# Moving the second half's norm, a spill of the residual and three weight tiles in a two-layer trunk on one Trainium2 core

## The reference

```python
x = x + g2[:, None, :] * y                      # end of layer 0
hk = _modulate(_rmsnorm(x, kv_norm_g), kv_shift, kv_scale)
k_all, v_all = jnp.split(hk @ kv_w, 2, axis=-1)
...
q = (h @ b_w_q[j]).reshape(B, S, N_HEADS, HEAD_DIM)
o = _stick_breaking(q, k_shared, v_shared)      # 16 heads of 64
y = o.transpose(0, 2, 1, 3).reshape(B, S, D) @ b_w_out[j]
x = x + g1[:, None, :] * y
```

## Time and profile before

| | |
|---|---|
| Time, median of 3 runs | 2663.4 us (2663.28 to 2665.89) |
| Profiled execution, its own time | 2662.75 us |
| Its span, first to last instruction | 2661.0 us |
| PE busy | 2573.8 us (97%) |
| DVE busy | 1438.4 us (54%) |
| ACT busy | 956.9 us (36%) |
| POOL busy | 149.4 us (6%) |
| Mean granted TensorE clock | 0.987 |

### The profile page before, as it was taken

How to read it: one execution, slowest core, us unless ns; L and a number is a source line. 1 busy time by engine, 2 the same in 40 slices (tenths; PEclk the granted TensorE clock), 3 DMA queues, 4 the chain that set the end, 5 groups by cost and what they waited for, 6 DMA issues and landing times.

```text
span 2661.0 us, 36194 instructions
## 1 busy us (share of the span) xinstructions
PE 2573.8 (97%) x13680; PEld 2159.2 (81%) x13680; DVE 1438.4 (54%) x1742; ACT 956.9 (36%) x1513; POOL 149.4 (6%) x152
## 2 busy tenths in 40 slices
PE   6999999999999999999999998999999999999999
PEld 4999998778888878888899886666688888888887
DVE  5436434447877655555532552777348656544442
ACT  5436222113654531111211232677426544411110
POOL 0000000000000000000000001666100000000000
PEclk9999999999999999999999998899999999999999
DMA  6321422223244474342222244555313332632311
GB/s 276 105 104 48 159 88 90 83 80 143 92 168 140 161 281 170 133 159 87 103 82 85 91 152 131 118 130 123 126 33 131 127 122 99 228 145 90 110 48 71
DMA packets 104778, 326.67 MB, mean 123 GB/s; under 512 B 10336, under 2 KB 26720, under 8 KB 100704
## 3 DMA queue, kind: packets, MB, share of 16 engines
q1 hardware_dynamic: 104672, 325.18, 36.2%
HBM read 253.84 MB, written 71.30 MB: 122 GB/s over the span
## 4 chain that ended last, share of the span: by engine, by line
PE 87%; DVE 6%; ACT 3%; DMA 2%; issue 1%; POOL 1%; SPq 0%; ACTq 0%; DVEq 0%; POOLq 0%
PE PS L1845 21%; PE PS L1847 21%; PE PS L1846 21%; PE PS L1949 5%; PE PS L1951 5%; PE PS L1950 5%; DVE KEEP L1767 2%; PE PS L2247 2%; PE PS L2260 1%; PE PS L2228 1%; ACT PS L1138 1%; PE PS L2184 1%; PE PS L2229 1%; DMA MOD<-in_modw 1%; DVE X L1421 1%
## 5 line engine op out<-in xcount | busy, mean ns | idle before, releaser
L1421 DVE SCALAR_TENSOR_TENSOR X<-PS,MODV,X 128x1024 f32<-128x1024 f32 x148 | 190.0, 1284 | 440.1 <-PE PS L1847 426.8
L1845 PE MATMUL PS<-HID_HI,W_HI 128*128 128x512 f32 x1024 | 400.5, 391 | 8.5 <-DVE HID_LO L1549 5.0
L1846 PE MATMUL PS<-HID_LO,W_HI 128*128 128x512 f32 x1024 | 399.1, 390 | 0.0
L1847 PE MATMUL PS<-HID_HI,W_LO 128*128 128x512 f32 x1024 | 398.9, 390 | 0.0
L387 ACT ACTIVATE W_HI<-RAW 128x1024 fp32r<-128x1024 f32 x146 | 152.1, 1056 | 597.8 <-PE PS L1847 497.4
L1949 PE MATMUL PS<-W_HI,H_HI 128*128 128x256 f32 x1216 | 348.3, 286 | 5.7 <-DVE H_LO L1259 5.7
L1950 PE MATMUL PS<-W_HI,H_LO 128*128 128x256 f32 x1216 | 346.0, 285 | 0.0
L1951 PE MATMUL PS<-W_LO,H_HI 128*128 128x256 f32 x1216 | 346.0, 285 | 0.0
L1949 PEld LDWEIGHTS PS<-W_HI,H_HI 128*128 128x128 f32 x1216 | 235.4, 194 | 9.0 <-DVE H_LO L1259 8.0
L1950 PEld LDWEIGHTS PS<-W_HI,H_LO 128*128 128x128 f32 x1216 | 235.6, 194 | 0.3 <-issue 0.2
L1951 PEld LDWEIGHTS PS<-W_LO,H_HI 128*128 128x128 f32 x1216 | 235.4, 194 | 0.0
(11 more groups left out here) (200 smaller groups left out, 4465.9 us busy)
## 6 DMA issues: line engine op xcount, KB each, us to landing
RAW<-in_wt SPq DMA_DIRECT2D x208, 512.0 KB, 3.6
MODRAW<-in_modw SPq DMA_DIRECT2D x96, 512.0 KB, 3.6
HRAW<-hid_scratch SPq DMA_DIRECT2D x14, 2048.0 KB, 9.9
hid_scratch<-TN SPq DMA_DIRECT2D x60, 256.0 KB, 2.8
hid_scratch<-SCR SPq DMA_DIRECT2D x56, 256.0 KB, 3.9
x_scratch<-X SPq DMA_DIRECT2D x3, 4096.0 KB, 12.0
X<-x_scratch SPq DMA_DIRECT2D x6, 2048.0 KB, 10.2
QK<-qk_scratch SPq DMA_DIRECT2D x16, 768.0 KB, 6.3
```

The lines of the kernel that those rows point to most:

```text
L1421: dve.scalar_tensor_tensor(X[:, k, :], flat(acc(u % 2)), MODV[:, gate + k:gate + k + 1], X[:, k, :], ALU.mult, ALU.add).then_inc(sem["acc_ ...
L1845: pe.matmul(dst, w_hi, m_hi, start=first, stop=False)
L1846: pe.matmul(dst, w_hi, m_lo, start=False, stop=False)
L1847: return pe.matmul(dst, w_lo, m_hi, start=False, stop=last)
```

## The change

Four edits. On DVE the three additions stand behind the copy of unit 0, `inverse` stands behind the copy of unit 2, and the eight pieces are made by twos behind the copies of units 3 to 6; before they were made by fours behind units 6 and 7. On PE `column_sums` follows unit 2 and `spread` unit 3, before units 3 and 5. On SP the spill of `X` is issued behind the store of unit 19, not ahead of all stores. At attention's end ACT and DVE cut tiles T_O and T_O+1 two and three steps into the last but one phase, T_O+2 in the last; SP loads T_O+2 and T_O+3 before the first half of `X`; and PE makes the first half of the first output unit (`first_o(0)`) before the last two `weigh` groups.

```diff
-            sp.wait_ge(sem["acc_free"], freed(U_KV_V - 1))
-            sp.dma_start(XD[:], X[:]).then_inc(sem["x_spilled"], 16)
...
                 sp.wait_ge(sem["acc_free"], freed(U_KV_V + u))
                 sp.dma_start(VD[2 * pair:2 * pair + 2, chunk].rearrange("h p d -> p h d"),
                              VST[:, u % 2, :, :]).then_inc(sem[f"vs_out{u % 2}"], 16)
+                if u == 19:
+                    sp.dma_start(XD[:], X[:]).then_inc(sem["x_spilled"], 16)
...
             load_raw(sp, Count(T_O))
             load_raw(sp, Count(T_O + 1))
+            load_raw(sp, Count(T_O + 2))
             sp.wait_ge(sem["z_full"], HEADS * STEPS)
+            load_raw(sp, Count(T_O + 3))
             sp.dma_start(X[:, 0:4, :], XD[:, 0:4, :]).then_inc(sem["x_back"], 16)
-            load_raw(sp, Count(T_O + 2))
-            load_raw(sp, Count(T_O + 3))
...
-                    if h.c >= HEADS and s in (4, 6, 8) and par == 0:
-                        cut_hi(act, Count(T_O + s // 2 - 2))
+                    if h.c >= HEADS and s in (2, 3) and par == 0:
+                        cut_hi(act, Count(T_O + s - 2))
+                    if h.c >= HEADS and s == 2 and par == 1:
+                        cut_hi(act, Count(T_O + 2))
...
             for u in range(16):
+                if u == 1:
+                    add_squares(2, 6, total(2, 1))
+                    add_squares(2, 7, total(2, 1))
                 v_store(u)
-                if u < 3:
-                    add_squares(2, 5 + u, total(2, 1))
-                if u == 4:
+                if u == 0:
+                    add_squares(2, 5, total(2, 1))
+                if u == 2:
                     inverse(2, 1)
+                if u == 3:
                     dve.wait_ge(sem["rs_full"], 6)
-                if u in (6, 7):
-                    pieces(2, 4 * u - 16, 4 * u - 12)
+                if 3 <= u < 7:
+                    pieces(2, 2 * u + 2, 2 * u + 4)
...
-                    if h.c >= HEADS and s in (5, 7, 9) and par == 0:
-                        cut_lo(dve, Count(T_O + s // 2 - 2))
+                    if h.c >= HEADS and s in (3, 4) and par == 0:
+                        cut_lo(dve, Count(T_O + s - 3))
+                    if h.c >= HEADS and s == 3 and par == 1:
+                        cut_lo(dve, Count(T_O + 2))
...
+                if u == 2:
+                    column_sums(2, 1)
                 if u == 3:
-                    column_sums(2, 1)
-                if u == 5:
                     spread(2, 1)
...
+            def first_o(half):
+                s, sl = T_O % RING, half_of(half)
+                if half == 0:
+                    pe.wait_ge(sem["w_lo"], tiles_cut(Count(T_O)).v)
+                    pe.wait_ge(sem["acc_free"], freed(U_O - 1))
+                    pe.wait_ge(sem["scanned"], HEADS * KT)
+                for k in range(8):
+                    if k == 7:
+                        pe.wait_ge(sem["o_lo"], 2 * KT - 1 + half)
+                    mm = three(PS[:, 2 * (U_O % 2) + half, :], W_HI[:, k, s * P:(s + 1) * P],
+                               W_LO[:, k, s * P:(s + 1) * P], OT_HI[:, k, sl], OT_LO[:, k, sl], k == 0, k == 7)
+                if half:
+                    mm.then_inc(sem["acc_full"], 1)
+
+            first_o(0)
             weigh(Count(KT - 1), STEPS - 2, 1)
             weigh(Count(KT - 1), STEPS - 1, 1)
-
-
-            pe.wait_ge(sem["o_lo"], 2 * KT)
+            first_o(1)
...
-            for j in range(4):
+            for j in range(1, 4):
                 wide_unit(Count(T_O + j), Count(U_O + j), OT_HI, OT_LO)
```

## The result

| | before | after |
|---|---|---|
| Time, median | 2663.34 us (2662.2 to 2665.89, 4 runs) | 2648.22 us (2646.36 to 2650.52, 4 runs) |
| Profiled execution, its own time | 2662.75 us | 2650.03 us |
| Its span | 2661.0 us | 2648.3 us |

The ratio after to before is 0.9942 [0.9925, 0.996]. The change gives 15.1 us where 11.5 were forecast. 2648.22 lies just inside the range, 0.2 us above its lower end of 2648.0, and outside rival A's own.

What follows compares the result with a forecast made beforehand. PE was taken to bound the kernel, through its waits and lower clock. Gains 8.8 - 2.4 - 0.9 + 6.0 = 11.5 us took 2662.75 to 2651.25; with 0.65 for the median the forecast was 2651.9 us, range 2648.0 to 2656.5.

Steps and rivals of the forecast that it cites:

- rival A: Whole kernel: the parts act as summed, 2651.9 us, own range 2649.5 to 2654.5; chance 0.58.
- What bounds the kernel: PE holds 87% of the chain of waits; time changes only where PE waits or works at the lower clock.
- Pieces earlier, 8.8 us: Border, units 7 to 9: pieces made earlier, unit 8 no longer waits, gain 8.8 us, lower bound 7.
- At its old place the spill cost PE nothing: Border, copy of unit 2: its wait for the store behind the spill goes and gives nothing, since unit 4 comes later.
- Spill behind unit 19: Unit 24: PE waits 2.4 us for stores behind the spill, plus 0.9 us for the clock.
- Rival B: Spill at its new place costs nothing, stores pass it or two buffers suffice: 2648.6 us; chance 0.12.
- the rule beside it: Trainium skill's queue-order rule at the spill: no store behind it reported before 1405.0, PE waits at least 1.6 us.
- Attention's end, 6.0 us: Attention's end: waits of 3.73 and 1.45 us and 2.4 of slow clock go, new wait 1.6; gain 6.0 us.
- The wait at `turn` 5: Attention's end: PE newly waits 1.6 us there for ACT's copy 2, which comes after the cut of T_O.
- The clock's price of 2.4 us: Attention's end: the slow stretch behind PE's 3.73 us wait goes, worth 2.4 us, bounds 1.5 and 2.95.
- The bounds of 3.5 and 6.9: Attention's end: lower and upper limits in us given for the gain of 6.0.
- Rivals C and E: Attention's end: C gives less, 2654.3 or to 2657 us, chance 0.16; E slower, low clock throughout, 2672.6, chance 0.04.

Runs made afterwards that it cites:

- e8: Kernel before with only the spill of X moved behind the store of unit 19; 2663.55 us, ratio 1.0001.
- e15: Kernel before with only the spill of X moved behind the store of unit 19, run once more; 2662.78 us, one run.
- e16: Kernel before with only the spill of X moved behind the store of unit 19, run yet again; 2660.22 us, one run.
- e14: Kernel before, unchanged, run again for its trace; 2665.83 us, one run.
- e3: Changed kernel with the spill of X back at its old place, ahead of all stores; 2645.42 us, ratio 0.9931.
- e7: Changed kernel with SP's old order at attention's end, X ahead of tiles T_O+2 and T_O+3; 2649.06 us, ratio 0.9947.
- e12: Changed kernel itself, run again; 2648.07 us, ratio 0.9944.

## Why the prediction was right or wrong

**What bounds the kernel: right.** Time was won only where PE waited or ran at the lower level.

**Pieces earlier, 8.8 us: right.** Units 7 to 9 lost what was read, and the new order gets it all back, with the slack that was forecast. With the spill out of the way the old order took 38.55 us with the clock fallen in units 0 and 1 (e8) and 36.4 with it held (e15, e16), the new one 29.7 and 28.2. So this edit is worth 8.9 or 8.2 us.

**"At its old place the spill cost PE nothing": the step that failed.** The prediction put this term at nothing. The runs show 5.7 us at the old place where the clock holds in units 0 and 1 (42.1 us with the spill there, 36.4 without), and 0.1 where it falls. The sentence said that the wait of the copy of unit 2 "goes and gives nothing", because unit 4 comes late enough. It looked at the next unit that needs the buffer and not at the third addition, which stood behind that copy on DVE and in front of the column sums on PE. Why it wasn't seen: the one profile of before has the clock fallen, and there the third addition ends at 1333.35 + 1.22 = 1334.57, just before PE comes to the column sums:

```profile
1333.35 1.22 DVE L1234 TENSOR_TENSOR TOT<-TOT,SQ 128x1024 f32<-128x1024 f32 x1
```

```profile
1334.62 1.95 PE L1858 MATMUL PS<-ONES,TOT 128*128 128x1 f32 x16
```

For that form the border's forecast is right, 38.6 against 29.7 us. In the other the old order took 42.1 us against 28.2, a gain of 13.9. Three terms make it up: 1.4 for PE's wait at the column sums, 6.8 x 0.45 = 3.1 for the clock behind it, and some 9.1 at units 7 to 9 (in e14 17.8 us from the copy of unit 6 to that of unit 9), together 13.6 of 13.9. The change removes this cost twice: the spill is elsewhere (e15 and e16 show that this alone does it), and all three additions now stand ahead of the copy of unit 1 (the first group of rows after). That the second alone would do too with the clock held is only argued: e3 was seen with the clock fallen.

How often is each form? Of the eighteen traces the clock fell in five and held in thirteen. With these shares the pieces give (5 x 8.9 + 13 x 8.2) / 18 = 8.4 us and the spill's old place (5 x 0.1 + 13 x 5.7) / 18 = 4.1, together 12.5. But of the five traces with the spill ahead of the stores it fell in three, of the thirteen others in two. If that is no chance, the old border takes (3 x 38.6 + 2 x 42.1) / 5 = 40.0 us in the mean and the new one (2 x 29.7 + 11 x 28.2) / 13 = 28.4, and the two edits together give 11.6. Five traces can't decide it.

**Spill behind unit 19: right.** A wait of 2.13 us for 2.4 (1.84 to 2.42 in eleven traces), and a clock that falls in seven of the eleven: 3.2 us in the mean for 3.3. Rival B (stores pass the spill) is out by the copy at 1398.04, released by its store. That no store could be reported before the spill's landing held here, but follows from the rule beside it only if the store runs on the engine that ends the spill last; no run shows which engines a store takes.

**Attention's end, 6.0 us: right in the sum, off in parts.** The wait at `turn` 5 was 1.47 us (1.6), and `first_o` is worth 1.45 (1.45). The clock's price of 2.4 us was that of one trace: of the seven traces with the old end, before and e15 had a low stretch of 6.8 us and took 203.2 and 202.9 us, the other five one of 3.4 us and took 201.5 to 201.9. The new end takes 196.7 to 197.0 (196.8 in the mean of the seven traces that have it unchanged, 196.70 in e7's), the old one 202.1 in the mean of seven. The gain is 6.5 against the profile and 5.3 in the mean. So the low clock was worth 2.8 us in the profile (6.5 + 1.5 - 3.73 - 1.45) and 1.6 in the mean. The bounds of 3.5 and 6.9 don't follow from the prediction's own terms, which give 5.1 and 6.5. Rivals C and E didn't come: in none of the nine traces that have the wait (1.42 to 1.71 us) did the clock fall behind it. Moving two tiles ahead of X did nothing (e7).

**The sum.** The forecast was -8.8 + 0 + 3.3 - 6.0 = -11.5 us. The traces give -8.4 - 4.1 + 3.2 - 5.3 = -14.6, or -11.6 + 3.2 - 5.3 = -13.7 by the second way to count; measured were -15.1 in the first comparison and -14.1 in e12's (2662.2 - 2648.07). Both sums lie within the noise of these. They are means over few traces, and the runs of one kernel spread by 2 to 9 us, so how often each form comes is known only roughly. What stays open is why the clock fell in units 0 and 1 in some traces and not in others: PE's waits for `H_LO` just ahead of it (1.03, 0.70 and 0.26 us) are the same in all eighteen, and what the spill's place has to do with it is open too.

## What to carry to other kernels

A wait on one engine that seems covered must be followed to every instruction behind it on that engine, not only to the next user of the buffer; here it was an addition behind the copy that paid. Where a stretch runs at the lower clock level in one profile, ask what would be late if it didn't, and take a second profile of the same kernel before pricing the stretch. A large transfer on a queue of small ones belongs where nothing behind it has a reader soon: here behind the last of the stores.

## What was unexpected of the hardware

The same program showed different clocks from run to run at the same instructions: at units 0 and 1 the clock fell in five of eighteen traces, behind the wait of 1.8 to 2.4 us at unit 24 in seven of eleven. A fall can save time elsewhere, because it makes PE late for a wait that is still to come (38.7 us against 42.1 in the kernel before). And the times of the kernel before spread over 7.1 us in all its runs, where the three of the first table of this document lay within 2.6; a single time couldn't have told any of the terms.
